# State-space results written back by halves of the batches, setup in 19 beats, first batch six beats later

## The reference

```python
mod = c_act @ w_ada[l] + b_ada[l]                 # shift, scale, gate
h = rms_norm(x, norm_g[l]) * (1 + scale) + shift
u, z_s, q, k, v, z_a = split(h @ w_in[l])         # w_in: 2048 x 6144
# s5_mixer (state-space part), 64 groups of 16 channels, 64 states each:
a_bar = exp(lam * exp(log_step));  b_bar = ((a_bar - 1) / lam) * b_mat
states = scan over 256 tokens of a_bar * s + b_bar @ u
y = gelu((c_mat @ states).real + d_skip * u)
a, b = split(y @ w_glu[l] + b_glu[l]);  y_s = a * sigmoid(b) * silu(z_s)
y_a = diff_attention(q, k, v) * silu(z_a)         # 8 heads
x = x + gate * (concat(y_s, y_a) @ w_out[l])
```

## Time and profile before

| | |
|---|---|
| median of 3 runs | 3323.19 us |
| the profiled execution, its own time | 3322.7 us |
| its span | 3320.9 us |
| PE busy | 3007.5 us (91%) |
| DVE busy | 2308.3 us (70%) |
| ACT busy | 1640.0 us (49%) |
| POOL busy | 323.9 us (10%) |
| mean granted TensorE clock | 0.947 |

### The profile page before, as it was taken

One profiled execution on the slowest core, in us unless ns is written; L12 is line 12 of the kernel. 1 busy time (PEld: TensorE's weight loads), 2 busy tenths in 40 slices (PEclk: granted clock), 3 DMA queues, 4 the chain that ended last, 5 costly groups with the idle time before them and its releaser, 6 DMA issues.

```text
span 3320.9 us, 59768 instructions
## 1 busy us (share of the span) xinstructions
PE 3007.5 (91%) x24092; PEld 2772.4 (83%) x24092; DVE 2308.3 (70%) x3580; ACT 1640.0 (49%) x2416; POOL 323.9 (10%) x569
## 2 busy tenths in 40 slices
PE   6799898889998998999899999699899999999987
PEld 2587777768888888998888888689899999999987
DVE  6467776677688867775666665767588855887565
ACT  3345554345465644744444442455555544555454
POOL 0012222100122230200000000000000000000000
PEclk8799999889999998999999998899999999999999
DMA  9876656664644454454232232345445555554543
GB/s 371 291 250 219 224 210 238 237 229 173 176 137 139 139 159 166 169 191 157 93 110 93 98 106 79 132 139 187 151 156 180 189 190 179 179 189 166 186 149 123
DMA packets 110708, 576.93 MB, mean 174 GB/s; under 512 B 33056, under 2 KB 33088, under 8 KB 46688
## 3 DMA queue, kind: packets, MB, share of 16 engines
q1 hardware_dynamic: 89040, 525.37, 45.1%
q0 software_dynamic: 20816, 44.27, 4.6%
q10 hardware_dynamic: 576, 3.47, 0.3%
HBM read 546.83 MB, written 17.83 MB: 170 GB/s over the span
## 4 chain that ended last, share of the span: by engine, by line
PE 63%; DVE 23%; ACT 6%; DMA 4%; issue 3%; POOL 1%; SPq 0%; DVEq 0%; ACTq 0%; POOLq 0%
PE acc L872 62%; DVE arena L832 7%; DVE rounded L832 5%; DVE upper L832 2%; ACT arena L869 2%; DVE arena L842 2%; ACT rounded L869 2%; DMA arena<-in_w_ada 2%; DMA arena<-in_w_in 1%; DVE upper L842 1%; ACT upper L869 1%; DVE upper L850 1%; PE acc L875 1%; DVE rounded L842 1%; DVE arena L838 1%
## 5 line engine op out<-in xcount | busy, mean ns | idle before, releaser
L872 PE MATMUL acc<-rounded 128*128 128x256 f32 x14832 | 1953.8, 291 | 70.6 <-issue 43.9
L872 PEld LDWEIGHTS acc<-rounded 128*128 128x128 f32 x14832 | 1862.0, 196 | 152.8 <-issue 111.4
L832 DVE TENSOR_TENSOR rounded<-arena,rounded 128x1024 fp32r<-128x1024 f32 (+1 forms) x832 | 1005.3, 1208 | 334.0 <-ACT rounded L869 266.2
L869 ACT ACTIVATE rounded<-arena 128x1024 fp32r<-128x1024 f32 (+1 forms) x864 | 883.7, 1023 | 657.2 <-PE acc L872 502.6
L872 PEld LDWEIGHTS acc<-upper_rounded,rounded 128*128 128x128 f32 x4416 | 546.1, 197 | 40.5 <-DVE rounded L832 20.9
L872 PE MATMUL acc<-upper_rounded,rounded 128*128 128x256 f32 x4416 | 553.8, 289 | 18.6 <-DVE rounded L832 18.5
L869 ACT ACTIVATE arena<-arena 128x256 f32<-128x256 f32 (+4 forms) x469 | 248.9, 531 | 302.6 <-DVE arena L832 210.9
L872 PE MATMUL acc<-arena 128*32 128x512 f32 (+7 forms) x1874 | 272.2, 475 | 88.8 <-DVE arena L832 46.3
L832 DVE TENSOR_TENSOR arena<-arena 128x256 f32<-128x256 f32 (+6 forms) x519 | 273.2, 526 | 52.0 <-ACT arena L869 30.3
L872 PEld LDWEIGHTS acc<-arena 128*32 128x32 f32 (+4 forms) x1874 | 126.0, 143 | 152.9 <-DMA arena<-in_w_ada 63.0
L842 DVE SCALAR_TENSOR_TENSOR arena<-arena 128x256 f32<-128x256 f32 (+5 forms) x461 | 205.7, 446 | 42.7 <-ACT arena L869 14.5
(11 more groups left out here) (88 smaller groups left out, 1137.0 us busy)
## 6 DMA issues: line engine op xcount, KB each, us to landing
arena<-in_w_in SPq DMA_DIRECT2D x164, 1024.0 KB, 5.0
arena<-in_w_ada SPq DMA_DIRECT2D x88, 1024.0 KB, 5.2
arena<-in_w_up SPq DMA_DIRECT2D x88, 1024.0 KB, 4.8
arena<-in_w_down SPq DMA_DIRECT2D x44, 1024.0 KB, 4.8
arena<-in_w_outa SPq DMA_DIRECT2D x16, 1024.0 KB, 7.0
arena<-in_w_glu SPq DMA_DIRECT2D x16, 1024.0 KB, 5.3
arena<-in_w_outm SPq DMA_DIRECT2D x16, 1024.0 KB, 5.1
arena<-in_w_out SPq DMA_DIRECT2D x16, 1024.0 KB, 4.9
```

The costliest lines, as they stand in the source:

```text
L832: return self.put(self.e and self.e.tensor_tensor(o, a, b, op))
L869: return self.put(self.e and self.e.activation(o, a, f, scale=scale, **kw))
L872: return self.put(self.e and self.e.matmul(o, l, r, start=start, stop=stop, skip_group_check=True))
```

## The change

- Setup: the 8 steps become 19 parts. In layer 0 nothing moves (all lie ahead of the first blocks with the same beats); in layer 1 there is one part each 8 blocks, so that they reach over `w_glu` and the first blocks of `w_outm` of layer 0, and `s5_first` and the preparation of batch 0 come after.
- The first batch waits six more beats after `u` is marked as loaded.
- A new generator `s5_back(l)` writes back batches 0 to 7 once they are done (in `w_in`, tiles 28 to 34), and batches 8 to 15 as before in `w_outa`; read-back is a step of its own (`s5_yr`); each `s5_out` is two parts, and a tile has 8 beats.
- Some tiles get places of their own in SBUF (`GS` for gelu, `QR`, `QI`); `upper` grows by 128 columns.

```diff
     def s5(self, l):
-        for i in range(8):
-            self.add("s5_setup", l, i)
-            yield
-            if l:
-                yield
+        for i, parts in enumerate((1, 2, 1, 4, 3, 2, 1, 5)):
+            for part in range(parts):
+                self.add("s5_setup", l, i, part)
+                if l or part == parts - 1:
+                    yield
+                if l:
+                    yield
...
         while ("u8", l, 0) not in self.marks:
+            yield
+        for _ in range(6):
             yield
...
-        self.add("s5_y", l)
-        for _ in range(20):
-            yield
-        for j in range(9):
-            self.add("s5_out", l, j)
-            yield
-            yield
-            if j:
-                self.add("part", ("ys", l), j - 1)
-            yield
-            yield
+            self.marks.add(("s5", l, b))
+
+    def s5_back(self, l):
+
+        for half in range(2):
+            while ("s5", l, 8 * half + 7) not in self.marks:
+                yield
+            self.add("s5_y", l, half)
+            for _ in range(14):
+                yield
+            self.add("s5_yr", l, half)
+            for _ in range(8):
+                yield
+            for j in range(4 * half, 4 * half + 4):
+                self.add("s5_out", l, j, 0)
+                for _ in range(3):
+                    yield
+                self.add("s5_out", l, j, 1)
+                for _ in range(2):
+                    yield
+                self.add("part", ("ys", l), j)
+                for _ in range(3):
+                    yield
...
-    def s5_y(l):
-        pool.wait_ge("s5_act", ("y", l, 15))
+    def s5_y(l, half):
+        pool.wait_ge("s5_act", ("y", l, 8 * half + 7))
         for q in range(8):
...
+            pool.dma(dst, V(U8 + 1024 * half, 32, 32, p0=16 * q, np_=16), f"s5_y8{half}", (l, q))
+
+    def s5_yr(l, half):
+        pool.wait_ge(f"s5_y8{half}", (l, 7))
+        src = m.scr_y[l, 512 * half:512 * half + 512].rearrange("(j p) t -> p j t", p=128)
+        pool.dma(V(U8 + 1024 * half, 4, 256), src, "s5_yt", (l, half))
```

More of the change, by code:

```diff
@@ L100 @@
 HALF = 1024
-N1, N2 = 25348, 11264
+N1, N2 = 25348, 11392
 NF = NS * 2 * HALF + 2 * 4096
@@ L1399, in part, with s5_setup @@
         act.act(to[0], V(src, 256), ACT.Copy).then_inc("part_act", key)
-    def s5_setup(l, i):
+    def s5_setup(l, i, part):
+        if part:
+            return
         if i == 0:
@@ L1440, in s5_run, with s5_out @@
                 act.act(V(to, 128), B(3, src, 128), ACT.Copy).then_inc("s5_act", (key, l, b))
-    def s5_out(l, j):
-        if j < 8:
-            s = TM + 256 * (j % 2)
+    def s5_out(l, j, part):
+        if part == 0:
             act.wait_ge("s5_dve", ("gelu", l, j))
-            act.act(V(s, 256), V(s, 256), ACT.Tanh).then_inc("s5_act", ("gelu", l, j))
+            act.act(V(GS, 256), V(GS, 256), ACT.Tanh).then_inc("s5_act", ("gelu", l, j))
     def att(l, h, i):
@@ L1777, in part, with s5_setup @@
         low(to, V(src, 256), key)
-    def s5_setup(l, i):
-        if i == 1:
+    def s5_setup(l, i, part):
+        if i == 1 and part == 0:
             dve.wait_ge("s5_act", ("step", l))
@@ L1804, in s5_setup @@
             dve.tt(V(P2, 576), V(P2, 576), V(PK, 576), MUL)
-        if i == 7:
+        if i == 7 and part == 0:
             dve.wait_ge("s5_act", ("trig", l, 2))
@@ L1814, in s5_setup @@
             dve.recip(V(T1, 64), V(T1, 64))
+        if i == 7 and part == 1:
             dve.tt(V(QR, 64), V(CO, 64), V(ARE, 64), MUL)
@@ L1822, in s5_setup @@
             dve.tt(V(QI, 64), V(QI, 64), V(T1, 64), MUL)
+        if i == 7 and part in (2, 3):
             p1, p2 = V(P1, (9, 64), (1, 8)), V(P2, (9, 64), (1, 8))
             qr, qi = V(QR, (1, 64), (0, 8)), V(QI, (1, 64), (0, 8))
[L1825 to L1828, removed]
+            one, two, op = ((p1, p2, ADD), (p2, p1, SUB))[part - 2]
+            at = PQ + 512 * (part - 2)
+            dve.tt(V(at, 64, 8), one, qr, MUL)
+            dve.tt(V(TM, 64, 8), two, qi, MUL)
+            dve.tt(V(at, 512), V(at, 512), V(TM, 512), op)
+        if i == 7 and part == 4:
             dve.memset(V(KS, 960, np_=16), 0.0)
@@ L1886, in s5_run, with s5_out @@
                    SUB).then_inc("s5_dve", ("sn", l, b))
[L1888 to L1896, removed]
+    def s5_out(l, j, part):
+        yj, sj, uj = V(U8 + 256 * j, 256), V(GS, 256), V(UT + 256 * j, 256)
+        if part == 0:
+            dve.wait_ge("s5_yt", (l, j // 4))
+            dve.stt(yj, uj, par("ssm_d", l * 8 + j), yj, MUL, ADD)
             dve.tt(sj, yj, yj, MUL)
@@ L1899, in s5_out @@
             dve.tt(sj, sj, yj, MUL).then_inc("s5_dve", ("gelu", l, j))
-        if j:
-            dve.wait_ge("s5_act", ("gelu", l, i))
-            dve.stt(V(UT + 256 * i, 256), s, 1.0, y, ADD, MUL).then_inc("s5_dve", ("out", l, i))
+        else:
+            dve.wait_ge("s5_act", ("gelu", l, j))
+            dve.stt(uj, sj, 1.0, yj, ADD, MUL).then_inc("s5_dve", ("out", l, j))
     def att(l, h, i):
```

58 lines of the change are left out of this document (37 added, 21 removed).

## The result

The changed kernel took 3301.07 us (median of 4 runs, 3296.36 to 3304.11); before, on the same chip, 3322.08 us (4 runs, 3320.02 to 3326.16). The ratio is 0.9934, with a 95% interval of 0.9917 to 0.9951: faster, by 21 us. The forecast was 3274 us, 49 us less than before. The same kernel measured again, with the later experiments, gave 0.9959 (0.9944 to 0.9974), 13.6 us. Both are far short of the forecast.

What follows compares the result with a forecast made beforehand. PE was taken as the bound by and large (63% of the chain), with wins only where it waits for DVE or transfers. 15 + 17 + 17 + 13 - 3 - 10 = 49 us off 3322.7 gave 3274 us; range 3256 to 3303.

Steps and rivals of the forecast that it cites:

- the half moved into `w_in`: Eight halves from tile 31 on: added DVE work charged at 6 and 4 us, 10 us in all (6 to 21).
- work of the same size: S5 steps of the six beats go to the far end, into `w_outa`, with no loss charged for them.
- first batch (tiles 0 to 7, both layers): Six beats' delay hides PE's wait for `u`, 7.37 and 7.69 us; gain 15 us (0 to 17).
- `w_outa` of layer 1: With half the tiles there, the stage falls from 67.1 to 50 us (48 to 57); gain 17 us.
- `w_outa` of layer 0: Tiles fit DVE's pace, waits for weights leave 7 of 24.5 us; gain 17 us (10 to 21).
- `w_glu` of layer 0: Setup spread from 8 halves over 19 relieves DVE; gain 13 us (8 to 18).
- `w_outm` of layer 0: Receives three setup parts and some of batch 0's preparation on DVE; loss 3 us (0 to 8).
- rival 1: Layer 0 stays tied to its weights: gains in `w_outa` and `w_glu` shrink from 30 to about 8; 3296 us, chance 0.18.
- the eight halves from tile 31 on near 44 us in layer 1: Sign in `w_in`: this window, 38.1 us before, would take near 44 us with the moved work.
- Rival 2: Gains come out whole: idle DVE time in `w_in` absorbs the moved work; 60 to 68 us, about 3258 us, chance 0.1.
- Rival 3: In `w_in` ACT waits in order before DVE's gelu, 32 us a layer come through; 3328 us, chance 0.06.
- Rival 4: Nothing gained: DVE near its limit everywhere, `w_outa` gains reappear in `w_in`, first batch's wait moves on; 3323 us, chance 0.04.

Runs made afterwards that it cites:

- tiles_late: The changed kernel with the first half still written and read back in `w_in`, but its four `s5_out` tiles moved to `w_outa`; 3281.94 us, ratio 0.9881.
- more_dve: The changed kernel with the square in the gelu argument done five times instead of once for the first half's tiles; 3319.73 us, ratio 0.9992.
- less_dve: The changed kernel with the gelu argument's DVE instructions cut for the first half's tiles, 12 fewer in each layer; 3296.3 us, ratio 0.9927.
- no_tanh: The changed kernel without ACT's Tanh and the waits on both sides of it for the first half's tiles; 3306.71 us, ratio 0.9957.

## Why the prediction was wrong

The failed step is "the half moved into `w_in`", with the sentence "I charge 6 and 4 us", and beside it the one on the six beats, "work of the same size". Together they charged 10 us for tiles 8 to 47; the two profiles of the change show 48.1 and 47.1.

| Step | Foreseen | Measured, first and second profile |
|---|---|---|
| first batch (tiles 0 to 7, both layers) | 15 | 13.6, 10.4 |
| `w_outa` of layer 1 (with `w_glu` of layer 1) | 17 | 19.1, 19.1 |
| `w_outa` of layer 0 | 17 | 13.5, 13.9 |
| `w_glu` of layer 0 | 13 | 16.1, 13.3 |
| `w_outm` of layer 0 | -3 | -3.6, -2.6 |
| tiles 8 to 47 of `w_in` | -10 | -48.1, -47.1 |
| sum | 49 | 10.6, 7.0 |

The five other terms came out within 4 us each in the first profile, so this is not a case of many small errors. That 3301 us lies in the stated range of 3256 to 3303 is luck. The upper end stood for rival 1, whose mechanism was not at work, and the second measurement, 3309 us, lies outside.

**First batch.** Right in its place: PE no longer waits for `u`, and the wait is hidden as worked out (three beats left 2.77 and 2.26 us). In layer 0 PE now stands 2.96 us for a `w_ada` unit just ahead of that place (at 164.93), where before it had no such wait. Wrong in its worth: the steps of the six beats were taken from tiles 0 to 7, where DVE has room (47.5 busy of 72.5 us), and pushed a batch's work against attention in tiles 8 to 47, where added work costs time. Alone they win 16 us in tiles 0 to 7 and lose 17 in tiles 8 to 47, and tiles_late with and without them can't be told apart. The prediction followed the steps only to the far end and not through the stretch between.

**`w_outa` and `w_glu`.** Right within 4 us each. In layer 1 the stage came out at 46.9 us, PE's own pace, against 50. DVE did not wait for the read-back: POOL wrote from 1242.59, asked for the half at 1250.51, and the first tile stands at 1261.32 without a wait. What was said of the transfer's size was wrong, though (below). One small slip: the six DVE times of a tile add up to 2.47 us, not 2.49, which changes nothing. Rival 1, layer 0 tied to its weights, fell: `w_outa` and `w_glu` of layer 0 gained 27 to 30 us, not 8.

**The moved half.** The earlier trace rows gave 5.8 and 9.2 us of free DVE time in eight halves, and the price was what did not fit. Three things were wrong with that.

- Busy time is not load. Each DVE instruction is followed by 0.04 us before the next can start: 59 of them are 2.4 us of the 5.8. The Trainium skill, "VectorE: DVE Perf Modes", section "The DRAIN you can't avoid", gives the drain behind an operation as roughly its duration less 266 ns. For a row of 0.42 us that would be 0.15 us, an estimate; the rows here have 0.04 us from end to start, and the rows decide.
- Not all that is idle can be used. On the chain that ended last DVE already had the eight halves before the change; the prediction used the chain of the whole kernel only. The chain in this window (before, 1072.7 to 1110.8):

```profile
by line: DVE arena L832 32.7%; DVE rounded L832 16.2%; DVE arena L842 6.8%; ACT arena L869 6.5%; issue 6.2%; DVE upper L832 5.7%; ACT rounded L869 5.6%; DVE arena L858 4.6%; PE acc L872 3.4%; DVE arena L854 3.0%; DVE arena L837 2.7%; PE acc
```

The DVE items shown come to 72%, PE's to 3.4%. Of the 3.4 us that remained 2.33 are one wait for ACT's part of a split. After the change a wait of the same kind is there again, and it is longer:

```profile
1090.99 0.43 DVE L832 TENSOR_TENSOR upper_rounded<-upper,upper_rounded 128x256 fp32r<-128x256 f32 x1 [2.33 <-ACT upper_rounded L869]
```

```profile
1090.85 0.42 DVE L850 TENSOR_TENSOR upper_rounded<-upper,upper_rounded 128x256 fp32r<-128x256 f32 x1 [3.23 <-ACT upper_rounded L887]
```

more_dve and less_dve show a price of about 1 us per us, so the price of 10 us of DVE and 24 gaps was 11 us a layer, not 5.

- The tiles cost more than their own time. In the 16 halves from tile 28 on DVE has 24 instructions and 11.3 us more (73.36 against 62.05 in tiles_late), with 1 us of gaps, and the stretch is 17.7 us longer (91.8 against 74.1). The 5.4 us beyond DVE's own 12.3 are more waiting of DVE, 13.2 us in place of 7.8. PE stood idle for 3.64, 1.99, 2.86 and 4.90 us there, among others. The granted clock, a mean over parts at 2.4 and at 1.2 GHz, is 0.87 in place of 0.98, and the same matmuls take 7.1 us more. How much of the 5.4 us comes from the clock and how much from the additional hand-overs between DVE and ACT was not separated. no_tanh, without these hand-overs, won 5.3 us in layer 1 and lost 2.6 in layer 0, in one profile each.

So 10 us became 30 for the tiles (13.7 and 16.1 by tiles_late), above the 21 that were named as the most, and the rest of the 48 is largely the six beats (8.8 and 8.1 alone, the first within noise). In `w_outa` the same tiles cost 7 us for both layers, so moving them there should win 23; by the medians tiles_late is 19 us faster than the first measurement of the change and 27 than the second. The sign that was named for this step, the eight halves from tile 31 on near 44 us in layer 1, looked almost kept at 46.0 (53.3 in layer 0). The fourth tile's DVE work starts at 1106.21, 1.7 us before that window ends, and more than half of the loss in layer 1 lies outside it.

**The other rivals.** Rival 2, that the idle DVE time of `w_in` takes the moved half in, is answered by the rows above. Rival 3 had the place right and not the price: ACT did stand before DVE's gelu argument, 13.1 us in four waits, but taking these away won nothing over both layers. Rival 4, DVE near its limit everywhere so that gains reappear in `w_in`, had 0.04, and its mechanism was the one at work for two of the terms. It deserved far more: the chain's 23% for DVE had to lie somewhere. In tiles 8 to 47 of layer 1 before, the five largest DVE items of the chain come to 43%.

## What to carry to other kernels

Before work is moved into a stretch because an engine is idle there for 15% of it, ask the chain that ended last, in that window, which engine holds it. If it is the engine that gets the work, charge each us in full, with its gap, and more if a stall lowers PE's clock. Put such work where the bound engine is another: the same four tiles cost 3.5 us in `w_outa`, where DVE stood at 34.6 of 46.9 us. And if a group of steps is delayed, follow it through every stretch that it crosses; here the wait removed at one end was about paid back in the middle.

## What the runs showed of the hardware

- Half the bytes did not come sooner. The transfers by issue, with their number, size and median time to landing, after:

```profile
scr_y<-upper POOLq DMA_DIRECT2D x32, 64.0 KB, 3.0
upper<-scr_y POOLq DMA_DIRECT2D x4, 512.0 KB, 7.6
```

and before:

```profile
scr_y<-upper POOLq DMA_DIRECT2D x16, 128.0 KB, 7.5
upper<-scr_y POOLq DMA_DIRECT2D x2, 1024.0 KB, 7.3
```

The read-back of 512 KB takes 7.6 us and that of 1 MB 7.3 us, while the writes of half the size take less than half. The prediction had taken the fixed part of the read-back for the smaller share; the runs don't show it so. The round trip of the second half is 7.9 us to the request and about 7.6 (the median) behind it, 15.5 us where 16 were taken. That the 16 came out is luck: the part up to the request fell from 17.0 to 7.9 us, more than by half, and the read-back not at all. By the Trainium skill, "DMA: Bandwidth & Descriptors", section "Anatomy of one DMA — SWDGE (gpsimd) path", the read-back would be 3.2 us, an estimate; the rows are over twice that, beside the stream of weights. What the difference is made of was not tested.
- An untouched stretch of 725 matmuls took anywhere from 64.4 to 72.9 us, with granted clocks of 1.00 to 0.86. A difference of 7 us between two profiles, a third of what was measured here, can come from this alone.
